# Second mixer: the long convolution's tap steps dealt out differently over the attention heads, its mean one head later, two weight splits moved

## The chip, the cores and the metric

The kernel runs on one core of one Trainium2 chip. The metric is the device time of one execution in microseconds (us); the time before is the median of three runs.

## What is computed

Two transformer blocks in sequence on x of 1 x 256 x 1024, all in float32. The change lies in the second block's mixer, which is a 31-tap depthwise convolution beside an attention with 12 heads of width 64 on 4 shared key/value groups (three branches: compressed, selected, window). Cut to what matters:

```python
def conv_mixer(a, w_dw, b_dw, ln_g, ln_b):
    u, v = jnp.split(a, 2, axis=-1)
    y = u * jax.nn.sigmoid(v)
    y = lax.conv_general_dilated(y, w_dw[:, None, :], window_strides=(1,),
        padding=[(CONV_WIDTH_2 - 1, 0)], ..., feature_group_count=CONV_CH) + b_dw
    y = layer_norm(y, ln_g, ln_b)
    return jax.nn.silu(y)

def compress(kr, pe, w1, w2):
    ...
    h = lo[:, :-1] + hi[:, 1:] + jnp.einsum("ld,ldh->h", pe, w1)
    return jnp.einsum("bngh,hd->bngd", jax.nn.silu(h), w2)
...
    s_c = jnp.einsum("bqgrd,bngd->bgrqn", qb, kc) - slopes * (...)   # compressed branch
    out = gb[..., 0:1] * o_c + gb[..., 1:2] * o_s + gb[..., 2:3] * o_w
...
    mix = jnp.concatenate([conv_out, nsa_out.astype(conv_out.dtype)], axis=-1)
    x = x + mix @ w_out
```

CONV_WIDTH_2 is 31 and CONV_CH is 256. Every dense product is taken at float32 accuracy as three products of a high and a low part.

## The kernel before

**Weights.** All dense products run on TensorE (PE) against weights that SyncE's queue loads in 1 MB pieces into four `raw` buffers, in the order of one list, `plan`. For product p, ScalarE (ACT) writes the high part `w_hi` (`high`, L1144), VectorE (DVE) the low part `w_lo` = raw - high (`low`, L1547), and PE multiplies three times per tile (`passes`, L601). There are three split buffers of each kind, so the splits run three steps ahead: `low_after(product_at[p])` makes DVE do the low part of the step that stands three behind p in the plan. A raw buffer is loaded anew once its low part is taken.

**The heads' loop.** The second mixer's tail is a loop `for h in range(QH + 3)` (QH = 12), written out once for each engine, and each engine keeps its own written order; semaphores join them. In head step h, PE turns the probabilities of head h-2 (`turn`, L867), makes the scores of head h (`scores`, L886 to L889), in even steps from 4 on attends two heads (`attend`, L906), then does the stages that `head_stages` lists for h, and last a large product or half of the first compression product, if `in2_heads` has one for h (0 vs, 1 q1, 2 kc, 3 and 4 the two halves of the compressed keys' first weights, 5 q2, 6 none, 7 vc, 8 and 9 the two halves of the compressed values' first weights). "vc" is the product of the values that are to be compressed.

**DVE in head step h** takes the row maxima of head h (`softmax`, L1933), normalises head h-1 (`normalise`, L1942 to L1951), does some steps of the convolution, its stages, and then `evacuate` of that head's product. A step of the convolution (`mixer_conv`, L1868) is one tap for both 128-channel tiles, two instructions over 128x256. There are 31 steps: 4 before the loop, then `TAPS_AT[h]` in step h, and from h = 7 on all that are left.

**Stages around the change.** "hidden0" (h = 6): PE turns the compressed keys' hidden values (L935), DVE copies a bias out (`cmp_pe_copy`, L1960), ACT applies Silu. "keys" (h = 7): PE makes the compressed keys (L944), DVE copies them (L2017, L2019). "mean": PE sums the convolution over the channels (L1002), which waits for all taps, DVE scales the sum and subtracts it (L1964, L1967), ACT squares. "c_scores" (h = 8): the compressed branch's scores on PE (L963), copied by ACT (L1430). "conv_norm" (h = 8): PE sums the squares (L1010), ACT takes the root (L1365), DVE inverts and scales (L1580, L1975, L1977), ACT applies Silu. PSUM banks 0 and 1 alternate over these stages and products in the order of the list, each use waiting for the one two before it to be read.

Of the kernel before, what the change touches and what calls it, by code (L numbers as in the profile page):

```python
# [70 lines left out]
def build(nc, a, out):  # L71
# [30 lines left out]
    with fixed:  # L102
# [115 lines left out]
        mean = conv_tmp[:, 0, :]  # L218
# [83 lines left out]
        product_at, raw_at = [], {}  # L302
# [20 lines left out]
        product_of = {}  # L323
# [169 lines left out]
        for name in in2_first:  # L493
            banks.use(name, *in2_free[name])
            if name == in2_first[2]:
                banks.use("rstd", rstd_col_set, 1)
        banks.use("vw1", *in2_free["vw"])
        head_stages = {6: ("hidden0",), 7: ("keys", "mean"), 8: ("c_scores", "conv_norm"), 9: ("c_softmax",),
                       10: ("conv_parts", "hidden1"), 11: ("c_turn", "values"), 12: ("out0", "out1"), 13: ("out2", "out3"), 14: ("out4",)}
        TAPS_AT = (2, 2, 2, 4, 4, 5, 6)  # L500
        stage_free = {"mean": (mean_set, 1), "conv_norm": (rms_set, 3), "hidden0": (cmp_hid_set, 2), "keys": (kc_set, 1), "c_scores": (c_copied2, 1), "c_softmax": (c_step, 2),
                      "hidden1": (cmp_hid_set, 4), "c_turn": (pc_set, 1), "values": (vc_set, 2)}
        heads_bank_free = dict(banks.last)
# [1013 lines left out]
        def vector_program(e):  # L1517
# [32 lines left out]
            def stream_to(i):  # L1550

                nonlocal plan_pos
                while plan_pos <= i:
                    kind, n, _ = plan[plan_pos]
                    if kind == "ada":
                        ada(n)
                    elif kind == "w":
                        low(n)
                    plan_pos += 1

            def low_after(i):
                n = step_of[i] + N_SPLIT
                if n < len(steps):
                    stream_to(steps[n])
# [17 lines left out]
            def pair(b):  # L1582
                return b[:].rearrange("p (k t) -> p k t", k=2)
# [68 lines left out]
            for p, (name, i) in enumerate(in1_order):  # L1652
# [11 lines left out]
                if 1 <= step <= HEADS:  # L1664
                    h = step - 1
# [206 lines left out]
            def go_on(work, n):  # L1872
                for _ in range(n):
                    next(work, None)

            def pair_tokens(which, name):
                dve.wait_ge(cmp_scaled, which + 1)
                if which:
                    dve.wait_ge(compressed, 2)
                for g in range(KV):  # L1880
                    src = cmp_raw[g % 2 * HD:(g % 2 + 1) * HD, g // 2, :].rearrange(
                        "p (c l two) -> p two l c", two=2, l=STRIDE // 2)
                    e.tensor_copy(cmp_in[0:HD, :, g, :], src[:, 0]).then_inc(cmp_paired_dve, 1)
                e.tensor_copy(cmp_in[:, :, KV, 0:2], cols(f"cmp_{name[0]}_pe_2", 0, CMP_LEN // 2).rearrange(
                    "p (s l) -> p l s", s=2)).then_inc(cmp_paired_dve, 1)

            def evacuate(name):
                p = product_of[name]
                b = bank[banks.bank[name]]
                src = pair(b)  # L1890
                if name == "cu":
                    dve.wait_ge(product_done, p + 2)
                    dve.wait_ge(rstd_set, 2)
                    e.tensor_tensor(conv_u, src, rstd_2, ALU.mult).then_inc(conv_scaled, 1)
                elif name == "cv":
                    e.tensor_tensor(conv_s, src, rstd_2, ALU.mult).then_inc(conv_scaled, 1)
                    dve.wait_ge(conv_sigmoid, 1)
                    dve.wait_ge(conv_scaled, 1)
                    e.tensor_tensor(conv_pad[:, :, PAD:], conv_u, conv_s, ALU.mult).then_inc(conv_padded, 1)
                elif name in ("ks", "kw"):  # L1900
                    k_, k_set = (ks_T, ks_set) if name == "ks" else (kw_T, kw_set)
                    dve.wait_ge(product_done, p + 1)
                    for half in range(2):
                        own_ = slice(half * HD, (half + 1) * HD)
                        t = e.tensor_tensor(k_[0:HD, half::2, :], src[own_], rstd_2[own_], ALU.mult)
                    t.then_inc(k_set, 1)
                elif name in ("q0", "q1", "q2"):
                    first = 4 * int(name[1])
                    dve.wait_ge(product_done, p + 1)
                    for half in range(2):  # L1910
                        own_ = slice(half * HD, (half + 1) * HD)
                        t = e.scalar_tensor_tensor(out=q2[0:HD, first + half:first + 4:2, :], in0=src[own_], scalar=INV_SQRT,
                                                   in1=rstd_2[own_], op0=ALU.mult, op1=ALU.mult)
                    t.then_inc(q2_copied, 1)
                elif name in ("kc", "vc"):
                    which = ("kc", "vc").index(name)
                    dve.wait_ge(product_done, p + 1)
                    if which:
                        dve.wait_ge(cmp_paired_act, KV)
                        dve.wait_ge(cmp_paired_dve, KV)  # L1920
                    e.tensor_tensor(cmp_raw, src, rstd_2, ALU.mult).then_inc(cmp_scaled, 1)
                    pair_tokens(which, name[0:1])
                if name not in ("cu", "cv", "vw", "vc"):
                    low_after(product_at[p])

            def softmax(h):
# [27 lines left out]
            def cmp_pe_copy(which):  # L1954
                src = bank[banks.bank[f"hidden{which}"]][:, 0:2 * P].rearrange("p (m g c) -> p m g c", m=2, c=N_CHUNKS)
                dve.wait_ge(cmp_turned, which + 1)
                if which:
                    dve.wait_ge(cmp_hid_set, 2)
                    dve.wait_ge(kc_made, 1)
                e.tensor_copy(cmp_pe[:], src[:, :, KV, 0]).then_inc(cmp_pe_set, 1)  # L1960
# [52 lines left out]
            def cmp_keys():  # L2013
                b = bank[banks.bank["keys"]]
                dve.wait_ge(kc_made, 1)
                dve.wait_ge(tables_pool, TABLES)
                e.tensor_copy(kc_wide[0:HD, :, KC_AT:KC_AT + N_CMP],  # L2017
                              b[0:HD, 0:KV * N_CMP].rearrange("p (g n) -> p g n", g=KV)).then_inc(kc_set, 1)
                e.tensor_scalar(kc_wide[HD:HD + 1, :, KC_AT:KC_AT + N_CMP],  # L2019
                                ext_i[HD:HD + 1, T:T + N_CMP].rearrange("p (o n) -> p o n", o=1).to_broadcast([1, KV, N_CMP]),  # L2020
                                0.5 * (CMP_LEN - 1), None, ALU.add).then_inc(kc_set, 1)
# [40 lines left out]
            for h in range(QH + 3):  # L2062
                if h < QH:
                    softmax(h)
                if 1 <= h <= QH:
                    normalise(h - 1)
                if h == 0:
                    low_after(product_at[product_of["vw"]])
                go_on(taps, TAPS_AT[h] if h < len(TAPS_AT) else TAPS2)
                if h == 8:  # L2070
                    low_after(product_at[product_of["vc"]])
                for stage in head_stages.get(h, ()):
                    if stage.startswith("hidden"):
                        if stage == "hidden1":
                            cmp_normalise()
                        cmp_pe_copy(int(stage[6]))
                    elif stage == "mean":
                        conv_mean()
                    elif stage == "keys":
                        cmp_keys()  # L2080
                    elif stage == "conv_norm":
                        conv_norm()
                    elif stage == "conv_parts":
                        dve.wait_ge(conv_hi, 1)
                        e.tensor_tensor(act_lo[:, 0:CT2, :], conv_acc, act_hi[:, 0:CT2, :].bitcast(F32),
                                        ALU.subtract).then_inc(conv_lo, 1)
                    elif stage == "c_softmax":
                        cmp_softmax()
                    elif stage == "values":
                        cmp_values()  # L2090
                    elif stage.startswith("out"):
                        head_sum(int(stage[3:]))
                if h in (12, 13):
                    head_low(2 * (h - 12))
                    head_low(2 * (h - 12) + 1)
                if h < len(in2_heads) and in2_heads[h]:
                    name = in2_heads[h]
                    if name == "w1k1":
                        low_after(raw_at[name])
                    elif not name.startswith("w1"):  # L2100
                        evacuate(name)
# [208 lines left out]
```

## Time and profile before

| | us |
|---|---|
| median of three runs | 761.5 (760.99 to 763.41) |
| profiled execution | 763.79 |
| its span, first to last instruction | 762.1 |
| mean granted TensorE clock over the span | 0.985 of full |

The profiled execution lies 2.3 us (0.3%) above the median; 1.7 us of it lie outside its span. A row of a timeline gives start, elapsed or busy time, engine, line, operation, result and operands and count, and in brackets how long the engine sat idle before it and what ended that. Where a row merges several instructions, its time runs from the first start to the last end.

### The profile page before, as it was taken

The page shows a single profiled execution, that of the slowest core. Times are in us where ns is not written, and L with a number is a line of the kernel's source. Part 1 is how long each engine was busy: PE and PEld are TensorE (multiplying, and loading weights), DVE is VectorE, ACT ScalarE, POOL GpSimd, SP SyncE. Part 2 cuts the span into 40 slices and gives each one's busy share as a digit, 9 for nine tenths or more (in the row PEclk, how much of TensorE's full clock was granted, in tenths as well). Part 3 has the DMA queues.
Part 4 walks back from the last instruction along what each step waited for, and adds up shares of the span by engine and source line. Part 5 has one row for each costly group of instructions (what it writes and reads, how often), then busy time and mean ns, then how long its engine had stood idle before and what let it go on. Part 6 is the DMA issues. An engine that isn't in the chain of part 4 may idle for free.

```text
span 762.1 us, 13431 instructions
## 1 busy us (share of the span) xinstructions
PE 729.0 (96%) x5817; PEld 694.0 (91%) x5817; DVE 513.9 (67%) x614; ACT 368.8 (48%) x508; POOL 70.8 (9%) x72
## 2 busy tenths in 40 slices
PE   5899999999999999999999999879899999999996
PEld 4799999999999999999999997767699999998884
DVE  4989688688565777754447978955875665656361
ACT  3444434453644544543435666357854635354341
POOL 1500111003000000000005000000000321331001
PEclk9899999999999999999999999979999999999999
DMA  9989866876605776785652651503164665664611
GB/s 344 374 275 348 274 198 208 282 283 219 219 31 170 238 252 225 233 264 172 214 174 65 216 166 56 166 1 106 61 221 152 227 202 185 204 200 159 201 48 55
DMA packets 118336, 146.49 MB, mean 192 GB/s; under 512 B 4005, under 2 KB 103557, under 8 KB 118277
## 3 DMA queue, kind: packets, MB, share of 16 engines
q1 hardware_dynamic: 116912, 143.58, 57.2%
q10 hardware_dynamic: 1364, 2.05, 0.8%
q8 instruction: 46, 0.75, 0.4%
q14 instruction: 14, 0.11, 0.1%
HBM read 144.57 MB, written 1.05 MB: 191 GB/s over the span
## 4 chain that ended last, share of the span: by engine, by line
PE 73%; DVE 17%; ACT 6%; issue 2%; DMA 1%; POOLq 0%; SPq 0%; DVEq 0%; ACTq 0%
PE bank L601 55%; PE bank L1100 8%; DVE w_lo L1547 6%; DVE mod_acc L1534 4%; ACT w_hi L1144 3%; PE bank L783 3%; DVE wide L1868 2%; DMA raw<-in_w_ada 1%; DVE wide L1817 1%; PE bank L661 1%; PE bank L638 1%; DVE score L1951 1%; DVE neg_max L1933 1%; PE bank L963 1%; ACT score L1404 1%
## 5 line engine op out<-in xcount | busy, mean ns | idle before, releaser
L1547 DVE TENSOR_TENSOR w_lo<-raw,w_hi 128x2048 fp32r<-128x2048 f32 x108 | 244.9, 2271 | 114.8 <-ACT w_hi L1144 114.5
L1144 ACT ACTIVATE w_hi<-raw 128x2048 fp32r<-128x2048 f32 x108 | 204.7, 1899 | 214.4 <-PE bank L601 164.6
L601 PE MATMUL bank<-act_hi,w_hi 128*128 128x256 f32 x816 | 229.1, 283 | 0.5 <-ACT act_hi L1301 0.2
L601 PE MATMUL bank<-act_lo,w_hi 128*128 128x256 f32 x816 | 226.6, 280 | 0.8 <-DVE act_lo L1606 0.5
L601 PE MATMUL bank<-act_hi,w_lo 128*128 128x256 f32 x816 | 222.8, 279 | 0.0
L601 PEld LDWEIGHTS bank<-act_hi,w_hi 128*128 128x128 f32 x816 | 155.1, 190 | 3.6 <-issue 2.7
L601 PEld LDWEIGHTS bank<-act_lo,w_hi 128*128 128x128 f32 x816 | 154.2, 189 | 1.8 <-DVE act_lo L1606 0.7
L601 PEld LDWEIGHTS bank<-act_hi,w_lo 128*128 128x128 f32 x816 | 152.1, 189 | 0.0
L601 PE MATMUL bank<-ffn_hi,w_hi 128*128 128x256 f32 x352 | 98.1, 279 | 0.0
L601 PE MATMUL bank<-ffn_hi,w_lo 128*128 128x256 f32 x352 | 97.4, 277 | 0.6 <-DVE w_lo L1547 0.6
L601 PE MATMUL bank<-ffn_lo,w_hi 128*128 128x256 f32 x352 | 97.3, 277 | 0.0
L601 PE MATMUL bank<-hidden_hi,w_lo 128*128 128x256 f32 x256 | 70.8, 277 | 0.9 <-DVE w_lo L1547 0.9
L601 PE MATMUL bank<-hidden_hi,w_hi 128*128 128x256 f32 x256 | 71.0, 277 | 0.0
L601 PE MATMUL bank<-hidden_lo,w_hi 128*128 128x256 f32 x256 | 70.7, 276 | 0.0
L601 PEld LDWEIGHTS bank<-ffn_hi,w_lo 128*128 128x128 f32 x352 | 66.2, 188 | 0.8 <-DVE w_lo L1547 0.8
L601 PEld LDWEIGHTS bank<-ffn_lo,w_hi 128*128 128x128 f32 x352 | 66.1, 188 | 0.1
L601 PEld LDWEIGHTS bank<-ffn_hi,w_hi 128*128 128x128 f32 x352 | 66.1, 188 | 0.1
L1534 DVE SCALAR_TENSOR_TENSOR mod_acc<-raw,col_tile,mod_acc 128x1024 f32<-128x1024 f32 x42 | 55.3, 1318 | 1.8 <-DMA raw<-in_w_ada 0.5
L2259 POOL TENSOR_TENSOR wide<-wide,rstd 128x512 f32<-128x512 f32 x11 | 28.9, 2627 | 246.0 <-ACT wide L1491 246.0
L601 PEld LDWEIGHTS bank<-hidden_hi,w_lo 128*128 128x128 f32 x256 | 48.1, 188 | 1.1 <-DVE w_lo L1547 1.1
L601 PEld LDWEIGHTS bank<-hidden_lo,w_hi 128*128 128x128 f32 x256 | 48.1, 188 | 0.0
L601 PEld LDWEIGHTS bank<-hidden_hi,w_hi 128*128 128x128 f32 x256 | 48.1, 188 | 0.0
(285 smaller groups left out, 1060.9 us busy)
## 6 DMA issues: line engine op xcount, KB each, us to landing
raw<-in_w_in SPq DMA_DIRECT2D x31, 1024.0 KB, 5.8
raw<-in_w_ada SPq DMA_DIRECT2D x24, 1024.0 KB, 7.2
raw<-in_w_gate_up SPq DMA_DIRECT2D x22, 1024.0 KB, 5.1
raw<-in_w_mlp_in SPq DMA_DIRECT2D x16, 1024.0 KB, 5.4
raw<-in_w_mlp_out SPq DMA_DIRECT2D x16, 1024.0 KB, 5.3
raw<-in_w_down SPq DMA_DIRECT2D x10, 1024.0 KB, 5.0
raw<-in_w_out SPq DMA_DIRECT2D x8, 1024.0 KB, 7.3
raw<-in_w_proj_conv SPq DMA_DIRECT2D x2, 1024.0 KB, 6.0
```

Source lines behind the costliest of these rows:

```text
L601: i = e.matmul(dst, lhs, rhs, start=start and k == 0 and (m == 0 or second is not None) and n == 0, stop=stop and k == kt - 1 and n == 2, ...
L638: i = e.matmul(o[:, k * HD:(k + 1) * HD], acc[:, k * P:(k + 1) * P], ones[:, 0:HD], start=True, stop=True, skip_group_check=True)
L661: t = e.matmul(bank[SUMS][:, tt * HD:(tt + 1) * HD], squares[:, k, tt * P:(tt + 1) * P], mean_of.to_broadcast([P, HD]), start=k == 0 and t ...
L783: t = e.matmul(o[:, m * T:(m + 1) * T], wp[:, k, cut], ap[:, k, :], start=k == 0 and m == 0 and n == 0, stop=k == kt - 1 and n == 2, skip_ ...
L963: t = e.matmul(b[0:C_ROWS, h // C_HEADS * T:(h // C_HEADS + 1) * T], kc_wide[:, h // PER_KV, at:at + C_ROWS], q2[:, h, :], start=(h == 0), ...
L1100: i = e.matmul(outs[tt][:, 0:n_cols], ap[:, k0 + k, own_], wp[:, k, :], start=first and k == 0 and n == 0, stop=last and k == kt - 1 and n ...
L1144: e.activation(w_hi[slot][:, 0:kt * n_cols], raw[i % N_RAW][:, 0:kt * n_cols], ACT.Copy).then_inc(hi_split, 1)
L1404: e.activation(score[par][:, at:at + keys], bank[S2_BANKS[tt]][:, br * keys:(br + 1) * keys], ACT.Exp, bias=neg_max[par][:, c:c + 1], accu ...
L1534: t = e.scalar_tensor_tensor(out=acc[:], in0=src[:, k, :], scalar=cols("c", r * ADA_TILES + k, 1), in1=acc[:], op0=ALU.mult, op1=ALU.add)
L1547: e.tensor_tensor(w_lo[slot][:, 0:kt * n_cols], raw[i % N_RAW][:, 0:kt * n_cols], w_hi[slot][:, 0:kt * n_cols].bitcast(F32), ALU.subtract) ...
L1868: e.scalar_tensor_tensor(out=conv_acc[:, j, :], in0=conv_pad[:, j, k:k + T], scalar=cols("conv_w_2", k * CT2 + j, 1), in1=conv_acc[:, j, : ...
L2259: e.tensor_tensor(s_, s_, rstd_2, ALU.mult).then_inc(gate_pool, 1)
```

## The change

`TAPS_AT`, the tap steps in head steps 0 to 6, goes from 2, 2, 2, 4, 4, 5, 6 (25 steps, with 2 left for h = 7) to 3, 4, 3, 2, 3, 2, 2 (19 steps, with 8 left for h = 7). The stage "mean" moves from the end of head step 7 to the start of the stages of head step 8, on PE, ACT and DVE alike, and so behind the product vc. The low part of q2's weights, which followed the evacuation of kc at the end of step 2, moves behind the normalising in step 3. The low part of the first output weights (OUT2), which followed the normalising in step 8, moves behind the mean in that step.

```diff
-        head_stages = {6: ("hidden0",), 7: ("keys", "mean"), 8: ("c_scores", "conv_norm"), 9: ("c_softmax",),
+        head_stages = {6: ("hidden0",), 7: ("keys",), 8: ("mean", "c_scores", "conv_norm"), 9: ("c_softmax",),
...
-        TAPS_AT = (2, 2, 2, 4, 4, 5, 6)
+        TAPS_AT = (3, 4, 3, 2, 3, 2, 2)
...
-                if name not in ("cu", "cv", "vw", "vc"):
+                if name not in ("cu", "cv", "vw", "kc", "vc"):
                     low_after(product_at[p])
...
-                if h == 0:
-                    low_after(product_at[product_of["vw"]])
+                if h in (0, 3):
+                    low_after(product_at[product_of["kc" if h else "vw"]])
                 go_on(taps, TAPS_AT[h] if h < len(TAPS_AT) else TAPS2)
-                if h == 8:
-                    low_after(product_at[product_of["vc"]])
                 for stage in head_stages.get(h, ()):
...
+                    elif stage == "c_scores":
+                        low_after(product_at[product_of["vc"]])
                     elif stage == "conv_norm":
                         conv_norm()
```

## Rows read from the trace of the kernel before

**Rows 1.** The page, part 1: busy us, share of the span, instructions.
```profile
PE 729.0 (96%) x5817; PEld 694.0 (91%) x5817; DVE 513.9 (67%) x614; ACT 368.8 (48%) x508; POOL 70.8 (9%) x72
```

**Rows 2.** Windows: length, busy PE, PEld, DVE, ACT, POOL, clock, DMA share, GB/s.
```profile
440.00:490.00 50.00, 48.73 (x365) 43.55 (x363) 43.05 (x96) 26.79 (x79) 0.00 (x0) 1.00 0.45 142
490.00:510.00 20.00, 13.76 (x75) 12.35 (x76) 11.83 (x35) 9.59 (x25) 0.00 (x0) 0.66 0.00 1
510.00:550.00 40.00, 37.60 (x263) 27.90 (x262) 28.79 (x72) 30.48 (x78) 0.00 (x0) 1.00 0.24 80
550.00:762.00 212.00, 204.07 (x1522) 192.57 (x1520) 119.62 (x100) 94.25 (x92) 30.94 (x12) 0.99 0.51 167
```

**Rows 3.** Timeline of PE, head steps 4 to 7.
```profile
470.19 0.87 PE L867 MATMUL bank<-ident,score 128*128 128x128 f32 x6 [0.59 <-DVE score L1951]
...
479.65 0.47 PE L601 MATMUL bank<-act_hi,w_hi 128*128 128x256 f32 x1
...
485.50 0.82 PE L867 MATMUL bank<-ident,score 128*128 128x128 f32 x6
...
487.32 0.59 PE L889 MATMUL bank<-kw_T,q 66*128 66x256 f32 x2
...
489.30 0.36 PE L935 MATMUL bank<-ident,wide 79*128 79x79 f32 x2
...
491.69 0.88 PE L867 MATMUL bank<-ident,score 128*128 128x128 f32 x6 [2.03 <-DVE score L1951]
...
497.10 0.65 PE L944 MATMUL bank<-cmp_hid,w2k 128*64 128x60 f32 x4 [1.74 <-issue]
...
500.57 2.07 PE L1002 MATMUL bank<-wide,ones 128*128 128x256 f32 x4 [2.82 <-DVE wide L1868]
```

**Rows 4.** Windows of 2 us around PE's wait in head step 7, columns as before.
```profile
490.00:492.00 2.00, 0.32 (x3) 0.32 (x4) 1.90 (x7) 1.98 (x8) 0.00 (x0) 1.00 0.00 0
...
492.00:494.00 2.00, 2.00 (x14) 1.91 (x12) 2.00 (x7) 0.69 (x1) 0.00 (x0) 0.69 0.00 0
...
506.00:508.00 2.00, 2.00 (x18) 2.00 (x17) 0.00 (x0) 0.15 (x1) 0.00 (x0) 0.89 0.00 0
```

**Rows 5.** Timeline of DVE, head steps 1 to 8.
```profile
448.77 0.42 DVE L1933 TENSOR_REDUCE neg_max<-bank 128x2 f32<-128x256 f32 x1 [1.51 <-PE bank L889]
...
455.47 1.39 DVE L1912 SCALAR_TENSOR_TENSOR q<-bank,rstd 64x512 f32<-64x512 f32 x2 [1.84 <-PE bank L601]
...
463.39 0.69 DVE L1921 TENSOR_TENSOR wide<-bank,rstd 128x512 f32<-128x512 f32 x1 [1.71 <-PE bank L601]
...
465.37 2.28 DVE L1547 TENSOR_TENSOR w_lo<-raw,w_hi 128x2048 fp32r<-128x2048 f32 x1
...
467.57 1.01 DVE L1933 TENSOR_REDUCE neg_max<-bank 128x2 f32<-128x256 f32 x2
...
470.06 3.25 DVE L1868 SCALAR_TENSOR_TENSOR wide<-wide,col_tile 128x256 f32<-128x256 f32 x8
...
491.55 4.83 DVE L1868 SCALAR_TENSOR_TENSOR wide<-wide,col_tile 128x256 f32<-128x256 f32 x12
...
496.30 0.15 DVE L1960 COPY cmp_pe<-bank 128x2 f32<-128x2 f32 x1
...
509.98 0.69 DVE L1921 TENSOR_TENSOR wide<-bank,rstd 128x512 f32<-128x512 f32 x1 [6.08 <-PE bank L601]
...
521.46 1.75 DVE L1580 RECIPROCAL wide<-rms 128x256 f32<-128x256 f32 x1 [4.73 <-ACT rms L1365]
```

**Rows 6.** Timeline of PE, head step 8.
```profile
509.78 0.82 PE L867 MATMUL bank<-ident,score 128*128 128x128 f32 x6
...
513.59 5.42 PE L963 MATMUL bank<-q,mod_acc 66*90 66x256 f32 x24
...
518.84 1.03 PE L1010 MATMUL bank<-wide,ones 128*128 128x256 f32 x4
```

**Rows 7.** Timeline of ACT, the copy of the compressed scores.
```profile
519.04 0.59 ACT L1430 ACTIVATE wide<-bank 90x512 f32<-90x512 f32 x1 [3.67 <-PE bank L963]
```

## Prediction

> **What bounds the kernel now.** I read the page first: PE is busy 96% of the span [rows 1], so time can only be won where PE stands still or runs slowly. The windows show where that is. Before and after the mixer's heads PE is as good as full; from 490 to 510 us it is busy 13.8 of 20 us, at a granted clock of 0.66 [rows 2]. DVE's share over the whole kernel, 67%, hides that DVE is the late engine just there.
>
> PE's timeline names the waits. PE leaves head step 6 at about 489.6 (the last stage, "hidden0", starts at 489.30), waits 2.03 us for the normalised scores of head 5, 1.74 us before the compressed keys, and 2.82 us for the convolution's last tap [rows 3]. The clock is at full up to 492, falls in the window after, and is back during 506 to 508 [rows 4]: half rate, 1.2 instead of 2.4 GHz, over some 14 us (by the means 0.69 and 0.89 of the two windows, from 492.8 to 506.4), of which the product vc's first part takes a share. vc ends at 509.78, when PE turns to step 8 [rows 6].
>
> DVE's timeline shows the cause. In steps 0 to 2 it waits for PE: 1.51, 1.84 and 1.71 us [rows 5]. Then it runs a backlog until about 503, and in it lie the taps of steps 3 to 7. While PE at last does vc, DVE stands idle for 6.08 us, and for 4.73 us more in step 8 [rows 5]. So DVE's work lies at the wrong places, and each microsecond by which it is late in steps 5 to 7 is one of PE's.
>
> **Prices.** Six tap steps take 496.30 - 491.55 = 4.75 us, so 0.79 each. The maxima and the normalising of a head take 470.06 - 467.57 = 2.49. A low split takes 467.57 - 465.37 = 2.20, the work on kc (and so on vc) 465.37 - 463.39 = 1.98, and q's evacuation about 1.4 [rows 5]. On PE a product takes 485.50 - 479.65 = 5.85, and an even head step with turn, scores and attend 489.30 - 485.50 = 3.80 [rows 3] (513.59 - 509.78 = 3.81 in step 8 [rows 6]). The compressed scores take 518.84 - 513.59 = 5.25, and from their end to DVE's reciprocal are 521.46 - 518.84 = 2.62, by way of ACT's copy [rows 5 to 7].
>
> **Steps 0 to 2: four taps more, at no cost.** One, two and one step more are 0.79, 1.58 and 0.79 us, and lie in idle stretches of 1.51, 1.84 and 1.71 [rows 5]. The evacuations after them still start when PE's products end. Without that cover they would cost 3.2 us of backlog.
>
> **Step 3: split of q2 later, two taps fewer.** After kc DVE goes straight to the maxima of head 3, at 465.4; they and the normalising end at 467.9 instead of 470.06. PE's wait of 0.59 us for them [rows 3] goes, and every later start of PE up to the product q2 is 0.6 earlier. The split follows at 467.9 to 470.1; the product q2 needs it at about 479 [rows 3], 9 us later, and nothing else is queued for it. The two taps end at 471.7.
>
> **Steps 4 and 5.** Each has its maxima and normalising, step 4 three taps (one fewer) and the low part of vc, step 5 two taps (three fewer). Step 4 runs 471.7 + 2.5 + 2.4 + 2.2 = 478.8, a wait for PE's scores of some 0.1 aside. Step 5: 478.8 + 2.5 + 0.4 of waiting for the scores + 1.6 = 483.3. DVE now stands before PE: q2's product ends at 485.50 - 0.6 = 484.9, and its evacuation takes DVE to 486.4.
>
> **Step 6.** PE's scores of head 6 end at 487.91 now [rows 3], so at 487.3. The second maximum and the normalising follow, and the turn of head 5 starts at about 489.6 instead of 491.69. PE is done with "hidden0" at 488.9 and idle for some 0.6 us instead of 2.03. Two taps (four fewer, 3.2 us) and DVE's copy for the Silu comes at 491.0 instead of 496.30 [rows 3, 5]. PE started the keys 0.80 after that copy, which is ACT's Silu: 491.8 instead of 497.10, and **5.3 us are won**.
>
> **Step 7.** With the mean gone from it, PE goes from the keys straight into vc. Now it takes 509.78 - 497.10 = 12.68 us from the keys to vc's end: the keys, 2.82 of waiting, the mean at half rate 2.07, vc partly at half rate [rows 3, 6]. Then it is 0.4 for the keys and 5.85 for vc, which ends at 498.05: **6.4 us won**. What makes this possible is the clock: PE has no gap above 0.6 us there, and the trace has such a gap at 469.6, of 0.59 [rows 3], with the clock at 1.00 over that whole window [rows 2]. DVE meanwhile: from 491.1, with 0.6 of waiting for the scores, 494.2; eight taps, 6.32 us, to 500.5; the keys' two copies to 501.0; the evacuation of vc and its pairs to 503.0. These eight steps lie beside vc, which ends before them, and beside the 3.8 us that PE has to do anyway.
>
> **Step 8.** PE does turn, scores and attend to 498.05 + 3.81 = 501.86. The mean needs the taps (500.5) and, by its PSUM bank, the keys' first copy (500.8): 1.1 us of slack. It takes 0.9 more here, to 502.75. The compressed scores need, by their bank, vc's first evacuation (501.7): 1.1 us of slack. They end at 508.0 instead of 518.84. The mean's cost is thus **0.9 us given back**. DVE: the maxima and normalising 503.0 to 505.5, the mean's three instructions to 506.7, ACT's squares by 507.4, 0.6 before PE wants them. Then the low part of OUT2, 506.7 to 508.9, in the time in which DVE waits for ACT's root; the reciprocal comes at 508.0 + 2.62 = 510.6 instead of 521.46. The split before the mean would have cost up to 2.2, so its place is what hides it. Its buffer is reloaded earlier than now, not later; ACT's high part of OUT2 no longer stands behind the squares.
>
> **After it** all engines have the same order with the same distances, 10.8 us earlier. The weights don't hold it: the DMA share is 0.24 from 510 to 550 and 0.51 afterwards [rows 2], and the loads wait for buffers, which come free with PE.
>
> **Sum:** 5.3 + 6.4 - 0.9 = **10.8 us**. The profiled execution would go from 763.8 to 753.0, its span from 762.1 to 751.3; it stands 2.3 above the median, so the median goes from 761.5 to **750.7**.
>
> **Bounds of what the trace doesn't show.** The gap of 0.6 at 489 may be nothing if DVE's handovers are shorter; then the best case, PE never waiting, is a further 0.8 us: 749.9. The slacks of 1.1, 1.1 and 0.6 us in step 8 rest on sums of nine DVE durations; if each head step on DVE runs 0.3 longer, DVE is 1.5 late and 0.9 is lost: 751.6. With 1 us for the spread of the runs below and the clock case above, that makes 748.8 to 754.8.
>
> **Rivals.** (A) *The clock still falls in step 6 or 7.* For it: turn, scores and "hidden0" are light work around the gap of 0.6, with a second small wait at the keys, and today the clock falls just after them [rows 4]. Against it: the gap of 0.59 at 469.6 without a fall. Price by the rows: the keys' extra 0.3, vc's 7.14 now (from the mean's end, 500.57 + 2.07, to 509.78 [rows 3, 6]) less 5.85, 1.3, and as much as 1.5 for scores of head 7, 3.1 in all: 753.8. The Trainium skill, "TensorE: Matmul & The Clock Gate", section "A second HAM failure mode: psum-queue depth-cycling", says that frequent short idle times between groups of matmuls make the clock swing between its two rates; by that rule case A holds, and here it speaks against a tightly packed step 7. The row at 469.6 does not bear it out for one such gap.
>
> (B) *DVE is still late in step 7.* Eight taps, the copies and vc's evacuation are one block of 8.8 us ahead of the mean and the compressed scores. If DVE reaches that block not at 494.2 but 3 us later, since some wait in steps 3 to 6 is not gone (the scores' exponentials on ACT, say), the compressed scores start about 2 us later as well as the keys 3 us: 10.8 - 3 to 5, so 754 to 756.
>
> (C) *No change.* The 10.8 us come back behind the heads, for a weight that isn't there. Speaks against it: DMA's share [rows 2]. It gives 761.5.
>
> (D) *Slower.* vc is the last heavy product before some 29 us of light work (turns, scores, 90-row products, transposes). If the time that is won lets PE's clock fall there, at the compressed scores in step 8, every microsecond of full-rate work costs one more. From 510 to 550 PE is busy 37.6 us at full rate [rows 2]; the case decides from 10.8 us of such work at half rate, and with 20 us of it the time is 761.5 - 10.8 + 20 = 771. Against it: the same work stands behind the same product today, and the clock is 1.00 over all of it.
>
> **How the numbers follow.** Forecast 0.72; A 0.11; B 0.08; C 0.05; D 0.04. 748.8 to 754.8 holds the forecast, nearly all of A and part of B, some 0.85. About 0.3% (2.3 us) is what a measurement of this kernel can tell from no change. Faster than that: the forecast, A and B, 0.91; within it: C, 0.05; slower: D, 0.04.
>
> **What would show it.** The windows from 484 to 510 at a granted clock of 1.00. DVE's copy for the Silu near 491, and no wait of PE above 1 us between the product q2 and the first output product. DVE idle near 483 for 1.6 us before q2's evacuation, and no idle of 6 us before vc's. The reciprocal of the normalisation near 510.6, and the end of the span near 751.3. Wrong would be: a fall of the clock after 489 (A), a wait for the taps or for vc's evacuation before the mean or the compressed scores (B), waits for weights behind 540 (C).

## The result, and the profile after

The changed kernel takes 750.96 us (median of four runs, 750.17 to 751.57); the kernel before, measured beside it, 761.25 (760.39 to 763.41). The ratio is 0.9844, with a 95% interval of 0.9803 to 0.9886. The forecast was 750.7, in a range of 748.8 to 754.8. The profiled execution took 751.52, its span 749.8. In another call, beside experiment 9, the changed kernel took 752.01 (751.44 to 752.58) against 761.90, a ratio of 0.9867. In several calls a few executions, of the kernel before as well, took some 7 to 10 us more than the rest at a mean clock of 0.968 to 0.979, and they are counted in the medians below.

The page of the changed kernel, parts 1 and 2: the busy time of each engine, and PE's granted clock in 40 slices.

```profile
PE 724.2 (97%) x5817; PEld 690.5 (92%) x5817; DVE 514.5 (69%) x614; ACT 368.9 (49%) x508; POOL 70.8 (9%) x72
...
PEclk9899999999999999999999999999999999999998
```

Part 1 has the same number of instructions for every engine. PE is busy 4.8 us less, 4.3 of them in the heads' stretch, where the low clock of 490 to 510 is gone: the same matmuls at full rate. The windows of the changed kernel (busy PE, PEld, DVE, ACT, POOL, clock, DMA share, GB/s) that answer to rows 2:

```profile
490.00:510.00 20.00, 20.00 (x132) 16.39 (x131) 17.18 (x43) 14.30 (x36) 0.00 (x0) 1.00 0.01 1
510.00:540.00 30.00, 27.59 (x211) 20.91 (x210) 23.78 (x58) 25.03 (x62) 0.00 (x0) 1.00 0.32 106
540.00:750.00 210.00, 201.78 (x1505) 190.28 (x1503) 117.65 (x100) 92.37 (x90) 30.92 (x12) 0.99 0.51 168
```

From 490 to 510 PE is busy in all 20 us at a clock of 1.00, where it had 13.8 at 0.66 [rows 2]. PE's timeline after, head steps 4 to 8 (rows 3 and 6 answer to it):

```profile
468.28 0.82 PE L867 MATMUL bank<-ident,score 128*128 128x128 f32 x6
...
488.39 0.87 PE L867 MATMUL bank<-ident,score 128*128 128x128 f32 x6 [0.72 <-DVE score L1951]
...
490.81 0.44 PE L944 MATMUL bank<-cmp_hid,w2k 128*64 128x60 f32 x4
...
496.95 0.82 PE L867 MATMUL bank<-ident,score 128*128 128x128 f32 x6
...
500.76 1.13 PE L1002 MATMUL bank<-wide,ones 128*128 128x256 f32 x4
501.73 5.34 PE L963 MATMUL bank<-q,mod_acc 66*90 66x256 f32 x24
506.91 1.03 PE L1010 MATMUL bank<-wide,ones 128*128 128x256 f32 x4
```

Of the waits of 0.59, 2.03, 1.74 and 2.82 us [rows 3] one of 0.72 is left. DVE's timeline after, steps 5 to 8 (rows 5 answer to it):

```profile
483.71 1.39 DVE L1912 SCALAR_TENSOR_TENSOR q<-bank,rstd 64x512 f32<-64x512 f32 x2 [1.83 <-PE bank L601]
...
489.84 0.15 DVE L1960 COPY cmp_pe<-bank 128x2 f32<-128x2 f32 x1
...
493.08 6.42 DVE L1868 SCALAR_TENSOR_TENSOR wide<-wide,col_tile 128x256 f32<-128x256 f32 x16
499.42 0.21 DVE L2017 COPY mod_acc<-bank 64x60 f32<-64x60 f32 x1
...
499.88 0.69 DVE L1921 TENSOR_TENSOR wide<-bank,rstd 128x512 f32<-128x512 f32 x1
...
505.47 2.29 DVE L1547 TENSOR_TENSOR w_lo<-raw,w_hi 128x2048 fp32r<-128x2048 f32 x1
...
509.52 1.75 DVE L1580 RECIPROCAL wide<-rms 128x256 f32<-128x256 f32 x1 [1.76 <-ACT rms L1365]
```

DVE waits for q2's product instead of PE waiting for DVE; the eight taps stand ahead of vc's evacuation, which waits for nothing (it was 6.08 [rows 5]).

**Counting from one mark.** Executions differ by up to 2.5 us before the heads begin: DVE's evacuation of q1 in step 1 (L1912) starts at 455.47 in the kernel before and at 454.31 in the changed one, with the same code up to there but for three tap steps more in idle time. The earliest of all, 452.97, is in a kernel with the old taps there (experiment 6), so this is no effect of the taps. So all traces are compared by the start of an operation less the start of that evacuation. "Head output" is the last L994 group, behind which the output products follow.

| us after q1's evacuation | keys L944 | vc's end (turn L867) | mean L1002 | compressed scores L963 | reciprocal L1580 | head output |
|---|---|---|---|---|---|---|
| before | 41.63 | 54.31 | 45.10 | 58.12 | 65.99 | 92.03 |
| changed | 36.50 | 42.64 | 46.45 | 47.42 | 55.21 | 81.25 |
| 1, taps alone | 37.33 | 54.00 | 46.06 | 57.81 | 65.68 | 91.71 |
| 2, mean alone | 41.41 | 49.93 | 53.74 | 54.71 | 62.50 | 88.54 |
| 3, taps and mean | 37.33 | 43.47 | 47.27 | 48.24 | 57.00 | 83.04 |
| 4, OUT2's split early | 36.50 | 42.44 | 46.25 | 47.22 | 56.18 | 83.33 |
| 5, six taps in step 6 | 39.52 | 45.63 | 49.44 | 50.40 | 58.20 | 84.21 |
| 5 again | 39.50 | 47.03 | 50.84 | 51.81 | 59.60 | 85.63 |
| 6, early taps back | 36.49 | 42.64 | 48.53 | 49.50 | 57.33 | 83.36 |
| 6 again | 36.50 | 42.44 | 48.54 | 49.50 | 57.34 | 83.39 |
| 7, before, PE kept busy | 41.57 | 51.71 | 45.09 | 55.51 | 63.38 | 89.40 |
| 8, four taps in step 5 | 36.31 | 42.25 | 46.06 | 47.03 | 54.82 | 80.86 |

Where equal work stands side by side, these numbers agree within 0.4 us, so smaller differences mean nothing. The changed kernel's heads are 10.78 us shorter; of the 12.3 between the spans 1.16 lie before q1's evacuation and 0.36 behind the heads, both within what traces of like kernels differ by.

### The profile page after: what moved, and what is told of

It is laid out like the page before. It is cut to its first block, busy times and chain, and to the rows that moved or that the text cites. A ratio compares the mean times of both kernels' runs of the same rounds, so it can differ in the third digit from the quotient of the medians.

```text
span 749.8 us, 13431 instructions
## 1 busy us (share of the span) xinstructions
PE 724.2 (97%) x5817; PEld 690.5 (92%) x5817; DVE 514.5 (69%) x614; ACT 368.9 (49%) x508; POOL 70.8 (9%) x72
## 4 chain that ended last, share of the span: by engine, by line
PE 89%; DVE 5%; ACT 3%; DMA 2%; issue 1%; POOLq 0%; SPq 0%; DVEq 0%; ACTq 0%
PE bank L601 68%; PE bank L1100 8%; PE bank L783 3%; DVE mod_acc L1534 2%; DMA raw<-in_w_ada 2%; PE bank L926 1%; PE bank L661 1%; PE bank L638 1%; PE bank L889 1%; PE bank L887 1%; PE bank L867 1%; PE bank L963 1%; DVE w_lo L1547 1%; PE bank L906 1%; ACT score L1404 1%
```

## The experiments

**1. The dealing of the taps alone**, on the kernel before:

```diff
-        TAPS_AT = (2, 2, 2, 4, 4, 5, 6)
+        TAPS_AT = (3, 4, 3, 2, 3, 2, 2)
```

> The kernel before with the new dealing of the taps alone; the mean stays in head step 7, ahead of the product vc, and both splits stay. Theory (the gain needs the taps and the mean's place together): the keys come some 4.6 us earlier, at about 492.5 on the clock of the trace before, but PE then waits about 8 us for the eight taps, mean and vc run at half rate as before, vc ends at about 510.4, 0.6 later than before. Time 761.3 to 762.5, no gain. Rival (the backlog of DVE ahead of the keys was the whole cost): half or more of the 10 us appears, 751 to 757.

Measured: 762.75, ratio 1.0024 (1.0000 to 1.0049). In its trace PE waits for the taps at the mean, ahead of vc:

```profile
499.58 2.08 PE L1002 MATMUL bank<-wide,ones 128*128 128x256 f32 x4 [8.29 <-DVE wide L1868]
```

The keys come 4.3 earlier (4.6 expected), the head output only 0.3, which is within the spread of the table. The granted clock falls during this wait, in the window 492 to 493 (0.75), so the mean takes 2.08 and vc starts at half rate, as in the kernel before. The backlog's removal ahead of the keys is worth nothing while the mean stands between them and vc.

**2. The mean's place alone**, on the kernel before:

```diff
-        head_stages = {6: ("hidden0",), 7: ("keys", "mean"), 8: ("c_scores", "conv_norm"), ...
+        head_stages = {6: ("hidden0",), 7: ("keys",), 8: ("mean", "c_scores", "conv_norm"), ...
```

> The kernel before with the mean moved to head step 8 alone; taps and splits as before. Theory: the keys stay at 497.1, the wait of 2.8 us and the mean at half rate go from the front of vc, vc still begins at half rate and ends near 504.9, the mean costs 0.9 behind it: 3.9 us won, 757 to 758. Rival (the mean's place is the whole gain): 752 or less.

Measured: 758.06, ratio 0.9961 (0.9946 to 0.9976); the head output is 3.5 earlier. As the theory had it (3.9 expected): the waits of 2.0 and 1.5 ahead of the turn and the keys stay.

**3. Taps and mean, both splits at their old places** (the edits of 1 and 2 together).

> Taps and mean as in the changed kernel, both splits at their old places. Theory: the gap of 0.6 on PE in step 4 is back, and DVE's split ahead of the mean puts the squares, the sums and the root later: PE's sums of squares wait about 1.6 us, the reciprocal comes 2.0 us later than in the changed kernel on the same count. 752.5 to 753.5, 2 us above the changed kernel. Rival (the splits are bystanders): 751.

Measured: 753.70, ratio 0.9904 (0.9882 to 0.9926); head output 1.8 behind the changed kernel's. PE's sums wait 0.93, not the 1.6 expected, with the clock at 1.00 from 506 to 514, and the reciprocal is 1.8 later (2.0). So taps alone give 0.3, the mean alone 3.5, both 9.0, and the splits add 1.8. Of these 0.8 are there at the keys already, by q2's split, and the other 1.0 come behind vc, by OUT2's.

**4. OUT2's split ahead of the mean**, on the changed kernel:

```diff
                 go_on(taps, TAPS_AT[h] if h < len(TAPS_AT) else TAPS2)
+                if h == 8:
+                    low_after(product_at[product_of["vc"]])
...
-                    elif stage == "c_scores":
-                        low_after(product_at[product_of["vc"]])
```

> The changed kernel with OUT2's split back ahead of the mean in step 8; q2's split stays moved. Theory: of the 2.2 us of the split 0.6 to 0.8 is slack, 1.4 to 1.6 shows: DVE's reciprocal at about 510.9 instead of 509.5, PE's sums wait about 1.5. Time 752.4. Rival (the wait for ACT's root hides it wherever it stands): 751.

Measured: 752.73, ratio 0.9883 (0.9866 to 0.9899). The reciprocal is 0.97 later, not 1.4, and the head output 2.08. The other 1.1 come with the clock: PE's sums of squares wait 1.12, and in the window around them the granted clock is 0.76 (1.00 up to 507, 0.50 from 508 to 511).

```profile
507.43 1.92 PE L1010 MATMUL bank<-wide,ones 128*128 128x256 f32 x4 [1.12 <-ACT wide L1424]
509.14 4.53 PE L926 MATMUL bank<-raw,cmp_in 128*79 128x256 f32 x16
...
505.00:510.00 5.00, 3.88 (x14) 2.46 (x13) 2.22 (x5) 3.08 (x6) 0.00 (x0) 0.76 0.00 0
```

The sums take 1.92 instead of 1.03, the compression's first half 4.53 instead of 3.62, together 1.8 more, of which 1.1 reach the head output. The total came out as expected, in another makeup. In 3 the same split stood in the same place, the wait was 0.93, and the clock did not fall.

**5. A gap put back on PE ahead of the keys**, on the changed kernel, twice:

```diff
-        TAPS_AT = (3, 4, 3, 2, 3, 2, 2)
+        TAPS_AT = (3, 4, 3, 2, 3, 2, 6)
```

> The changed kernel with six taps in head step 6 instead of two, and so four instead of eight left beside vc. It puts a gap of about 2.9 us back on PE ahead of the keys. Theory (the gap costs its length and the clock as well): keys at 493.8 instead of 490.81, the granted clock falls near there, the first part of vc runs at half rate, 1.3 us more: vc ends 4.6 us later, 755.6. Rival (waiting is all, the clock stays): 754.1. Rival (the time is hidden behind something else): 751.

> The kernel with six taps in head step 6 once more: its first trace had a gap of 2.92 us on PE ahead of the keys and a granted clock of 1.00 through it. Theory (whether a gap of this length brings the clock down depends on the moment at which it falls, not on its length alone): either outcome, and a trace with a fall would be 1 to 2 us longer at vc's end (47 instead of 45.6 us after q1's evacuation). Rival (gaps of up to 3 us never bring it down here): the trace is the same as the first.

Measured: 756.06, ratio 0.9949 (0.9910 to 0.9989), and again 755.96, ratio 0.9923 (0.9883 to 0.9963). The two traces show the same gap and two outcomes. First the keys and the windows of the first, then those of the second:

```profile
494.59 0.41 PE L944 MATMUL bank<-cmp_hid,w2k 128*64 128x60 f32 x4 [2.92 <-issue]
...
492.00:494.00 2.00, 0.00 (x0) 0.00 (x0) 2.00 (x7) 0.02 (x1) 0.00 (x0) 1.00 0.00 0
...
496.00:498.00 2.00, 2.00 (x20) 2.00 (x19) 2.00 (x6) 2.00 (x10) 0.00 (x0) 1.00 0.04 12
```

```profile
493.40 0.41 PE L944 MATMUL bank<-cmp_hid,w2k 128*64 128x60 f32 x4 [2.93 <-issue]
...
494.00:496.00 2.00, 2.00 (x12) 2.00 (x12) 1.97 (x6) 1.99 (x7) 0.00 (x0) 0.56 0.00 0
496.00:498.00 2.00, 2.00 (x13) 2.00 (x12) 2.00 (x7) 2.00 (x7) 0.00 (x0) 0.59 0.06 12
```

The first trace contradicts my theory (vc's end 3.0 later, the gap alone), the second bears it out (4.4). Length alone does not decide whether the clock falls. What does decide it these runs don't show.

**6. The taps of steps 0 to 2 back at the old places**, on the changed kernel, twice:

```diff
-        TAPS_AT = (3, 4, 3, 2, 3, 2, 2)
+        TAPS_AT = (2, 2, 2, 2, 3, 2, 2)
```

> The changed kernel with the old 2, 2, 2 taps in head steps 0 to 2 and so twelve instead of eight left for step 7. Theory: the four taps in steps 0 to 2 were free, at the end of step 7 they are not: 3.2 us more of DVE work ahead of vc's evacuation against a slack of 1.1, so PE waits some 2 us at the mean and the compressed scores, and DVE's reciprocal comes 2.4 later. 753.4. Rival (the tap steps beside vc are hidden whatever their number): 751.

> The kernel with 2, 2, 2 taps in head steps 0 to 2 and twelve left for step 7, once more, since its first timed runs scattered from 753.7 to 768.7 while its trace showed 2.1 us. Theory (the 2.1 us of the trace are all): 753 to 754. Rival (these twelve taps cost more than the trace showed): 757 or more.

Measured: 759.19, ratio 0.9935 (0.9891 to 0.9978), and again 758.45, ratio 0.9924 (0.9884 to 0.9963). Both traces show just the expected: PE waits about 2 us at the mean, the head output is 2.1 later, and the clock is 1.00 in every window from 484 to 560. The rows of the first and the second run:

```profile
502.89 1.13 PE L1002 MATMUL bank<-wide,ones 128*128 128x256 f32 x4 [2.02 <-DVE mod_acc L2017]
```

```profile
501.51 1.13 PE L1002 MATMUL bank<-wide,ones 128*128 128x256 f32 x4 [2.22 <-DVE mod_acc L2017]
```

But the medians are over 5 us above what these traces show. Each execution is listed with its mean granted clock. Over both runs six took 752.1 to 754.0 at 0.990 to 0.993, one 755.8, and eleven 758.3 to 760.6 at 0.981 to 0.984 (the other four took 767 to 769). Two of nine in the first run and four of nine in the second are quick ones, so how often each outcome comes is open. Both profiled ones are of the first group. So the rival that these taps cost more than the trace shows is right for eleven of eighteen executions, and in them the mean clock is lower: from 0.992 to 0.982 is 0.010 x 755 x 2 = 15 us more at half rate. That the lower clock is what costs the 5 us is likely and not shown. In the kernel before, in the call of the first run, executions at 0.982 took 761.0 to 761.9 and those at 0.988 and 0.989 took 759.8 to 761.4: some 10 us more at half rate went with less than 1 us there by the medians of the two, so what such time costs depends on what PE has to do in it. Where in the kernel the 15 us lie no trace shows, as both profiles caught the quick group; the light stretch behind the mean is a guess.

**7. The kernel before, PE kept busy in its three waits**:

```diff
+                if h == 7:
+                    keep_busy(8, start_bank("keys"))
...
                 b = start_bank("keys")
+                keep_busy(6, b)
...
                 b = start_bank("mean")
+                keep_busy(11, b)
```

> The kernel before, with 25 small matmuls on the identity whose result nobody reads, put into PE's three waits of head step 7 (8 before the turn, 6 before the keys, 11 before the mean). Nothing else moves. Theory (of the 10.8 us the half clock is a part): the granted clock stays at 1.00, the mean takes 1.0 instead of 2.07 and vc 5.85 instead of 7.14, DVE's dates stay: 2.3 us won, 759.0. Rival (the clock costs nothing, the waits hide it): 761.3.

Measured: 760.21, ratio 0.9993 (0.9958 to 1.0028): the times can't tell it from no change. The trace can. PE with the added matmuls (L670), and one window:

```profile
489.33 1.99 PE L670 MATMUL bank<-ident 128*128 128x128 f32 x16
491.50 0.87 PE L867 MATMUL bank<-ident,score 128*128 128x128 f32 x6 [0.18 <-DVE score L1955]
...
496.87 0.44 PE L945 MATMUL bank<-cmp_hid,w2k 128*64 128x60 f32 x4 [1.54 <-ACT cmp_hid L1324]
...
500.39 1.13 PE L1004 MATMUL bank<-wide,ones 128*128 128x256 f32 x4 [0.42 <-DVE wide L1872]
...
494.00:498.00 4.00, 2.46 (x22) 2.21 (x22) 3.90 (x13) 1.68 (x3) 0.00 (x0) 1.00 0.02 4
```

The clock stays at 1.00 from 484 to 512, through a wait of 1.54 that the added matmuls left ahead of the keys. Keys and mean come when they came (41.57 and 45.09), vc ends 2.6 earlier, and so does the head output. Between these two traces that is the clock's share of the 10.8; the rest is waiting. The medians lie only 1.0 apart, 760.21 against 761.17, so over many executions the share may be smaller.

**8. Four taps in step 5**, on the changed kernel:

```diff
-        TAPS_AT = (3, 4, 3, 2, 3, 2, 2)
+        TAPS_AT = (3, 4, 3, 2, 3, 4, 2)
```

> The changed kernel with four taps in head step 5 instead of two, six left for step 7. Theory: DVE stands idle for 1.83 us there before q2's evacuation, so the two taps fit, PE is what sets the order from step 3 to the mean, and nothing changes: 751.0, while DVE's end of the taps comes 1.6 us earlier. Rival (DVE still sets the time in step 7 or 8): 749.5.

Measured: 751.22, ratio 0.9857 (0.9791 to 0.9923). DVE's two rows: its wait for q2 shrinks from 1.83 to 0.24, and it is done with the taps 1.8 earlier after the mark, to no one's use: the head output is 0.4 earlier, no more than the table's spread.

```profile
483.63 1.39 DVE L1912 SCALAR_TENSOR_TENSOR q<-bank,rstd 64x512 f32<-64x512 f32 x2 [0.24 <-PE bank L601]
...
497.74 0.21 DVE L2017 COPY mod_acc<-bank 64x60 f32<-64x60 f32 x1
```

**9. A version to beat the changed kernel:** ACT's high part of the second output weights goes into ACT's idle time in step 7. The changed kernel ran beside it once more (10).

```diff
                 if name not in ("cu", "cv"):
                     high_after(product_at[p])
+                if name == "vc":
+                    high_after(raw_at["w1v0"])
...
-                        if name != "w1v1":
+                        if name[2] == "k":
                             high_after(raw_at[name])
```

> The changed kernel with ACT's high part of the second output weights moved from head step 8, behind the convolution's Silu, to step 7, where ACT stands idle for 4.37 us before vc's pairs. It takes 1.9 us off ACT's chain ahead of head 9's exponentials, which PE's scores of head 10 wait for. Theory: 0.5 to 1.3 us won, 750.0 against the changed kernel in the same call. Rival (those waits of PE are covered by other ones): no change.

> The changed kernel once more, as the measure for the run beside it on the same chip: 751.0.

Measured: 750.86 (750.62 to 751.05), ratio 0.9849 (0.9834 to 0.9864), and the changed kernel 752.01 (751.44 to 752.58), ratio 0.9867 (0.9850 to 0.9883). The medians lie 1.15 apart and the ranges of four runs each don't meet, but the intervals of the ratios overlap, and the changed kernel's first measurement had the same median, 750.96. So the times don't show a gain; the traces show a small one. ACT with the moved split, two in a row ahead of its wait in step 7, and head 9's first exponential:

```profile
494.46 3.74 ACT L1144 ACTIVATE w_hi<-raw 128x2048 fp32r<-128x2048 f32 x2
...
515.55 0.37 ACT L1406 ACTIVATE score<-bank,neg_max 128x128 f32<-128x128 f32 x1
```

and the same exponential in the changed kernel beside it:

```profile
517.29 0.37 ACT L1404 ACTIVATE score<-bank,neg_max 128x128 f32<-128x128 f32 x1
```

It is 1.8 us earlier after the mark, and the head output 0.76 (80.11 against 80.87; 0.5 to 1.3 were expected): part of ACT's 1.9 was PE's wait.

## Why the prediction was right

**The diagnosis** held: DVE's dates were PE's waits. 1 and 2 show that the two edits need each other, 0.3 and 3.5 against 9.0 together.

**Steps 0 to 2** (four taps at no cost): the evacuations still follow PE's products at once, and 6 shows the price of not using that idle time: 2.1 in the traces, as 3.2 less a slack of 1.1 has it, and more in most executions.

**Step 3:** the wait of 0.59 is gone (turn at 468.28 without one), back as 0.60 in 3. Forecast 0.6.

**Step 5:** DVE's wait for q2 is 1.83; from the forecast's own dates, 484.9 less 483.3, it was to be 1.6. 8 shows that it is real slack.

**Step 6:** keys 5.13 earlier (5.3), PE's gap 0.72 (0.6). The forecast dated the keys by ACT's Silu, 0.80 after DVE's copy. In the changed kernel the Silu is done at 490.54 and PE starts the keys at 490.81 without a wait, straight from its own turn and scores, which take 2.42 from 488.39. This step of the forecast had another path than the kernel took; from its own 489.6 for the turn the keys would have come at 492.0, and this is the 0.2.

**Step 7:** from the keys to vc's end 12.68 - 6.14 = 6.5 us less (6.4), the clock at 1.00. Of these 2.6 are the clock's, by the trace of 7.

**Step 8:** the mean costs 47.42 - 42.64 less the old 3.81, 1.0 (0.9). The slacks: the keys' first copy ends at 499.63, the mean starts at 500.76, so 1.1 (1.1); vc's evacuation ends at 500.57, the compressed scores start at 501.73, so 1.2 (1.1). The squares were done 0.9 ahead of the sums (0.6). The split of OUT2 behind the mean saves 1.0 of reciprocal, by 4 and by 3, where "up to 2.2" stood.

**The sum:** 10.8 forecast, 10.78 in the heads' stretch (5.13 + 6.54 - 0.97 = 10.70, and 0.08 behind). That the two agree so closely is partly luck: the terms are off by 0.1 to 0.2 each, and by the medians the gain is 10.3, and 9.9 in the second call. The profiled execution was forecast at 753.0 and came at 751.52; the difference is mostly the 1.16 before the heads, which the forecast couldn't know. The lower bound, 749.9 less 1, comes to 748.9 and not 748.8, and nothing hangs on it.

**The rivals.** A (the clock falls) did not occur in the changed kernel, but its mechanism is alive: 4 and 5 show it at gaps of 1.12 and 2.93. The argument that I used against it rested on a single gap of 0.59. It held: eleven traces have a gap of 0.71 or 0.72 at this turn, and in each the clock was 1.00 from there up to PE's next gap of more than 0.72. For longer gaps it would have been wrong as a rule. The Trainium skill, "TensorE: Matmul & The Clock Gate", section "A second HAM failure mode: psum-queue depth-cycling", has frequent short idle times between groups of matmuls make the clock swing. The changed kernel's trace, with a gap of 0.72 and a clock of 1.00, doesn't bear that out, nor do its four gaps of 0.59, 0.42, 0.41 and 0.49 between 522 and 529, also at 1.00; in 4 the clock fell around a single gap of 1.12, which fits it only in part. B needed DVE to reach the block of step 7 3 us late, and no run tested just that; 6 made the block itself 3.2 us longer, which cost 2.1 in the traces, and 7.6 in the median of the eighteen executions. C: the DMA share behind the heads is 0.51 as before, and PE has no new wait there. D, the slower case, was priced as light work at half rate behind vc. It did not occur in the changed kernel, but 4 shows a piece of it (1.8 us of extra time in the sums and the first compression half), and 6, with PE's gap in just that step, has its group of executions at 0.982. Even that group, 758.3 to 760.6, stays below the median of the kernel before.

## What to carry to other kernels

When one engine's backlog and another engine's wait meet at a point, look for the idle time of the late engine a few steps before and behind, and move its work there; check whether a step that needs the work's end (here the mean) can stand behind the next big product, because either edit alone may give little or nothing. Write down the slack that each wait keeps: here 2.1 us over it cost 2.1 in the traces, and 7 to 10 in most executions, at a lower mean clock. To compare traces of one kernel family, count from a mark just before the change, since what lies before it differed by up to 2.5 us from execution to execution.

## What the runs showed that I had not expected

The granted clock fell around a gap of 1.12 us (4). It stayed up through gaps of 2.02 and 2.22 (6) and of 2.92 (5), and the same kernel's gap of 2.93 brought it down in the next profile. So the same code has more than one outcome: a gap that costs 2.1 us in two traces (6) goes with eleven of eighteen executions 7 to 10 us above the changed kernel's 750.96, with mean clocks of 0.981 to 0.984, where the profiled executions have 0.990 and 0.993, and the changed kernel 0.991 to 0.994 in its eight runs. One profile of such a kernel shows one of its outcomes only; the list of clocks by execution showed the others.
